# Gate and up projections of a two-block language model: one 512-column matmul in place of two of 256 columns, with the two halves of the bank added by VectorE

## The reference, cut to what matters

```python
def swiglu(h, w_gate_up, w_down):          # h: (1, 256, 1024)
    gu = h @ w_gate_up                     # 1024 x 5632
    gate, up = jnp.split(gu, [D_FF], axis=-1)        # D_FF = 2816
    return (jax.nn.silu(gate) * up) @ w_down         # 2816 x 1024

h = h + hybrid_mixer(rmsnorm(h, norm_mix_w[l]), ...)
h = h + swiglu(rmsnorm(h, norm_ffn_w[l]), w_gate_up[l], w_down[l])     # for l in 0, 1
```

## Time and profile before

| | before |
|---|---|
| median of 3 runs | 2579.13 us (2577.0 to 2579.67) |
| profiled execution, its own time | 2580.57 us |
| span from first to last instruction in it | 2578.8 us |
| PE busy | 2251.0 us (87%) |
| VectorE busy | 1209.9 us (47%) |
| ScalarE busy | 923.3 us (36%) |
| mean granted TensorE clock | 0.947 |

### The profile page before, as it was taken

One profiled execution on the slowest core, in us unless ns is written; L12 is line 12 of the kernel. 1 busy time (PEld: TensorE's weight loads), 2 busy tenths in 40 slices (PEclk: granted clock), 3 DMA queues, 4 the chain that ended last, 5 costly groups with the idle time before them and its releaser, 6 DMA issues.

```text
span 2578.8 us, 37982 instructions
## 1 busy us (share of the span) xinstructions
PE 2251.0 (87%) x16798; PEld 1689.4 (66%) x16798; DVE 1209.9 (47%) x1715; ACT 923.3 (36%) x1315; POOL 1.4 (0%) x6
## 2 busy tenths in 40 slices
PE   8998676667989666676999999999999999999998
PEld 7773122112744221121899999989989999898997
DVE  3543212121873111110565588665456647876554
ACT  4141000001232000000555577554345546865443
POOL 0000000000000000000000000000000000000000
PEclk9999878788999888888999999999999999999999
DMA  7419999999258999999644443445444444344542
GB/s 287 165 58 395 427 428 428 427 428 427 117 249 360 428 428 427 428 427 427 266 164 164 168 159 136 164 179 188 171 180 164 164 150 182 142 154 164 184 176 106
DMA packets 48203, 662.94 MB, mean 257 GB/s; under 512 B 5344, under 2 KB 5600, under 8 KB 7968
## 3 DMA queue, kind: packets, MB, share of 16 engines
q1 hardware_dynamic: 47808, 659.17, 63.6%
q0 software_dynamic: 224, 1.26, 0.1%
HBM read 659.36 MB, written 1.05 MB: 256 GB/s over the span
## 4 chain that ended last, share of the span: by engine, by line
PE 59%; DMA 27%; DVE 6%; ACT 6%; issue 1%; DVEq 0%; SPq 0%; ACTq 0%
DMA ring<-w_dram 27%; PE ps L2476 8%; PE ps L2478 8%; PE ps L2477 8%; PE ps L1932 3%; PE ps L891 3%; PE ps L1355 2%; PE ps L2732 2%; PE ps L2733 2%; PE ps L2734 2%; PE ps L923 2%; PE ps L3340 2%; PE ps L3338 2%; PE ps L3339 2%; ACT r L2453 1%
## 5 line engine op out<-in xcount | busy, mean ns | idle before, releaser
L2464 DVE TENSOR_TENSOR r<-ring,r 128x1024 fp32r<-128x1024 f32 (+2 forms) x376 | 503.9, 1350 | 352.3 <-ACT r L2453 351.7
L2476 PE MATMUL ps<-r 128*128 128x256 f32 x2112 | 607.7, 288 | 5.6 <-DVE r L2536 5.5
L2477 PE MATMUL ps<-r 128*128 128x256 f32 x2112 | 598.6, 283 | 0.0
L2478 PE MATMUL ps<-r 128*128 128x256 f32 x2112 | 598.4, 283 | 0.0
L2453 ACT ACTIVATE r<-ring 128x1024 fp32r<-128x1024 f32 (+2 forms) x376 | 428.5, 1155 | 290.7 <-PE ps L2478 126.9
L891 PE MATMUL ps<-ring 128*32 128x512 f32 x1936 | 298.9, 750 | 180.9 <-DMA ring<-w_dram 180.7
L2476 PEld LDWEIGHTS ps<-r 128*128 128x128 f32 x2112 | 405.2, 192 | 12.3 <-issue 7.3
L2477 PEld LDWEIGHTS ps<-r 128*128 128x128 f32 x2112 | 405.4, 192 | 0.5
L2478 PEld LDWEIGHTS ps<-r 128*128 128x128 f32 x2112 | 405.3, 192 | 0.0
L891 PEld LDWEIGHTS ps<-ring 128*32 128x32 f32 x1936 | 61.4, 124 | 405.1 <-DMA ring<-w_dram 200.9
L1137 DVE TENSOR_TENSOR arena<-ps,arena 128x512 f32<-128x512 f32 x16 | 11.1, 692 | 440.0 <-PE ps L891 440.0
(11 more groups left out here) (446 smaller groups left out, 3067.2 us busy)
## 6 DMA issues: line engine op xcount, KB each, us to landing
ring<-w_dram SPq DMA_DIRECT2D x301, 2048.0 KB, 22.8
arena<-w_dram SPq DMA_DIRECT2D x6, 2048.0 KB, 13.9
ring<-w_dram SPq DMA_DIRECT2D x4, 1024.0 KB, 4.9
arena<-w_dram SPq DMA_DIRECT2D x2, 1536.0 KB, 7.2
x<-x_dram SPq DMA_DIRECT2D x2, 512.0 KB, 3.8
ring<-w_dram SPq DMA_DIRECT2D x2, 512.0 KB, 10.3
out_dram<-x SPq DMA_DIRECT2D x4, 256.0 KB, 2.0
cst<-w_dram SPq DMA_DIRECT2D x1, 973.0 KB, 23.4
```

What stands on the lines that cost most here:

```text
L2464: v.tensor_tensor(lo, w, hi.bitcast(F32), SUB).then_inc(*S.up(f"lo {s}", *(["free " + name] if last else [])))
L2476: pe.matmul(out, hi[:, k, :], K.HH[:, k, :], start=k == 0, stop=False)
L2477: pe.matmul(out, hi[:, k, :], K.HL[:, k, :], start=False, stop=False)
L2478: r = pe.matmul(out, lo[:, k, :], K.HH[:, k, :], start=False, stop=k == 7)
```

## The change

Upper and lower features of a block k become one moving operand of 512 columns (`K.HHL`, a view of the same buffer: two pieces of 256 columns that lie 2048 elements apart). `wide_pe` takes a bank for each tile instead of one for each pair. Its matmul of `hi` by `HHL` writes the whole bank: `hi` by `HH` in the left half, `hi` by `HL` in the right half. `lo` by `HH` is added to the left half by a second matmul of 256 columns. PE doesn't add the two halves; `wide_dve` does, with a copy of the right half to SBUF and an addition of the left half to it, for each tile, with a wait on VectorE's own semaphore between the two. Gate and up thus both pass through VectorE into `FF`, where before ScalarE read the gate and VectorE the up part straight from PSUM. Silu now waits for VectorE's sum of the gate (`g{i} sum`) and reads SBUF, the sums of up wait for Silu, because they overwrite `FF`, and the product is a third pass over `FF` in SBUF, behind one more wait on VectorE's own semaphore. The wait for `f{i-2}` stands now on VectorE as well (its own signal of two chunks ago). ScalarE's wait for `nT6 read` in chunk 0 goes. No transfer is added, taken away or moved in the order.

```diff
--- before.py
+++ after.py
@@ -223,6 +223,7 @@
         self.TMP = sb("tmp", 1536)
         self.CSR = sb("csr", 288, F32R)
         self.HH, self.HL = (R32[:, i * 2048:(i + 1) * 2048].rearrange("p (k t) -> p k t", k=8) for i in range(2))
+        self.HHL = R32[:, 0:4096].rearrange("p (h k t) -> p k h t", h=2, k=8)
         self.WS = [[R32[:, i:i + 2048].rearrange("p (k n) -> p k n", k=8) for i in (j, j + 2048)]
                    for j in (4096, 8192)]
         self.ps = ctx.enter_context(nc.psum_tensor("ps", [128, 8, 512], F32))
@@ -2492,6 +2493,30 @@
             yield
 
 
+def wide_pe(K, pe, S, j, name, first=None):
+
+    for n in range(2):
+        p = bank(K, pe, f"{name}{n}")
+        hi, lo = parts(K, j + n)
+        pe.wait_ge(*K.after(f"lo {j + n}"))
+        for k in range(8):
+            if first and n == 0:
+                wait_features(K, pe, first, k)
+            pe.matmul(half2(p), hi[:, k, :], K.HHL[:, k, :, :], start=k == 0, stop=False)
+            r = pe.matmul(p[:, 0:256], lo[:, k, :], K.HH[:, k, :], start=False, stop=k == 7)
+        r.then_inc(*S.up(f"used {j + n}", f"{name}{n}"))
+
+
+def wide_dve(K, v, S, out, name):
+
+    for n in range(2):
+        p = K.banks[f"{name}{n}"]
+        v.wait_ge(*K.after(f"{name}{n}"))
+        v.tensor_copy(out[:, n, :], p[:, 256:512]).then_inc(*S.up())
+        v.wait_ge(*S.now())
+        v.tensor_tensor(out[:, n, :], p[:, 0:256], out[:, n, :], ADD).then_inc(*S.up(f"{name}{n} read", f"{name} sum"))
+
+
 def proj_beside(K, e, S, j, cut, todo=(), fine=False, last=None):
 
     for n in range(2):
@@ -3320,8 +3345,7 @@
     for i in range(11):
         c = K.first_tile[f"{st}_gu{i}"]
         for j, part in ((0, "g"), (2, "u")):
-            for _ in proj_pe(K, pe, S, c + j, f"{st} {part}{i}", first=None if i or j else st):
-                pass
+            wide_pe(K, pe, S, c + j, f"{st} {part}{i}", first=None if i or j else st)
     acc = {(t, n): bank(K, pe, f"{st} d{t}{n}") for t in range(2) for n in range(2)}
     for i in range(11):
         if i % 2 == 0:
@@ -3350,15 +3374,13 @@
         c = K.first_tile[f"{st}_gu{i}"]
         for _ in proj_beside(K, a, S, c, cut_act):
             pass
-        a.wait_ge(*K.after(f"{st} g{i}"))
+        a.wait_ge(*K.after(f"{st} g{i} sum"))
         if i > 1:
             a.wait_ge(*K.after(f"{st} f{i - 2}"))
-        elif i == 0:
-            a.wait_ge(*K.after(f"{st} nT6 read"))
-        a.activation(b.SG[i % 2], half2(K.banks[f"{st} g{i}"]), ACT.Silu).then_inc(*S.up(f"{st} g{i} read"))
+        a.activation(b.SG[i % 2], b.FF[i % 2], ACT.Silu).then_inc(*S.up(f"{st} silu{i}"))
         for _ in proj_beside(K, a, S, c + 2, cut_act):
             pass
-        a.wait_ge(*K.after(f"{st} u{i} read"))
+        a.wait_ge(*K.after(f"{st} ff{i}"))
         a.activation(b.FH[:, 2 * i:2 * i + 2, :], b.FF[i % 2], ACT.Copy).then_inc(*S.up(f"{st} fh{i}"))
     for i in range(11):
         if i % 2 == 0:
@@ -3372,12 +3394,17 @@
     norm_HL_dve(K, v, st, st + "_gu0")
     for i in range(11):
         c = K.first_tile[f"{st}_gu{i}"]
+        FF = b.FF[i % 2]
         for j in (0, 2):
             for _ in proj_beside(K, v, S, c + j, cut_dve):
                 pass
-        v.wait_ge(*K.after(f"{st} u{i}"))
-        v.wait_ge(*K.after(f"{st} g{i} read"))
-        v.tensor_tensor(b.FF[i % 2], half2(K.banks[f"{st} u{i}"]), b.SG[i % 2], MUL).then_inc(*S.up(f"{st} u{i} read"))
+            if i > 1 and not j:
+                v.wait_ge(*K.after(f"{st} f{i - 2}"))
+            elif j:
+                v.wait_ge(*K.after(f"{st} silu{i}"))
+            wide_dve(K, v, S, FF, f"{st} {'gu'[j // 2]}{i}")
+        v.wait_ge(*S.now())
+        v.tensor_tensor(FF, FF, b.SG[i % 2], MUL).then_inc(*S.up(f"{st} ff{i}"))
         v.wait_ge(*K.after(f"{st} fh{i}"))
         f = slice(2 * i, 2 * i + 2)
         v.tensor_tensor(b.FL[:, f, :], b.FF[i % 2], b.FH[:, f, :].bitcast(F32), SUB).then_inc(*S.up(f"{st} f{i}"))
```

## The result

The changed kernel takes 2585.05 us (median of 20 runs, 2580.31 to 2589.22), the kernel before, run beside it, 2580.82 us (20 runs). The ratio of the two on record is 1.0015, 95% interval 1.0009 to 1.0022: 3.9 us slower, between 2.3 and 5.7 (the plain difference of the medians is 4.2). Slower was forecast, with 7.1 us. The sign and the mechanism hold; the size was 1.8 times what was measured. Twenty runs of each kernel still tell it from nothing.

What follows compares the result with a forecast made beforehand. The VectorE-ScalarE chain, 12.03 us a chunk against PE's 11.31, was to become the bound; with the seam each stage ends 3.56 us late, 2 x 3.56 = 7.1 us, so 2586.2 us, range 2577 to 2593.

Steps and rivals of the forecast that it cites:

- PE's gain: Matmuls of gate and up in ffn0 and ffn1: 0.353 us a block, not 0.360; 2.35 us a stage, 4.7 for both.
- The chain: VectorE and ScalarE taking turns in each gate-and-up chunk: 12.03 us start to start, against PE's 11.31.
- PE's start after a late cut: PE's first matmul behind a wait for VectorE's cut was to start 0.33 us after the cut's end.
- When it bites: Gate-and-up chunks: each eats 0.72 us of PE's slack, which lasts four chunks; from chunk 6 PE waits in each.
- the cushion: PE's slack at tile 7, between the end of VectorE's cut and PE's arrival: 3.2 us.
- Start of the down projection: PE was to start down 0 at 1843.14 us, 1.17 us behind before.
- The seam: Passage to the down projection: chunk 10's evictions delay double-tile cuts; PE 0.83 us later at down 1, 3.56 late at down 2.
- covered turn-taking: Rival: chain under 11.67 us stays hidden, kernel not slower; 2574.4 us, or 2576.4 with a seam cost; chance 0.10.
- free own waits: Rival: VectorE's waits for its own results cost nothing; chain 11.45 us, only the seam remains, 2576.4 us; chance 0.06.
- a slower PE: Rival: the two-piece moving operand slows PE's matmuls; at 0.40 us a block 14 us a stage, 2607 us; chance 0.04.
- The longer chain: Rival: VectorE's small operations take 0.48 us each; chain 12.47 us a chunk, 2595.6 us; chance 0.15.
- the second rival: The rival of free own waits: five times 0.11 us off the chain, said to come to 11.45 us; chance 0.06.

Runs made afterwards that it cites:

- wide_left: Changed kernel's 512-column matmuls, but Silu and product read only the left halves straight from PSUM, right halves left out of the result; ratio 0.9963 to the kernel before.
- all3: Changed kernel with both copies before both additions, ScalarE's cut of tile 4i+5 before Silu, down 1 and 2 cut early; ratio 0.9970 to the kernel before.
- inter: Changed kernel, but for each pair of tiles VectorE does both copies, then both additions; ratio 0.9971 to the kernel before.
- all3b: The kernel all3 run once more, for its interval; ratio 0.9972 to the kernel before.

## Why the prediction was right, and where its size was off

- *PE's gain*: forecast 0.353 us a block, 2.35 us a stage. Measured in the changed kernel 0.347 in ffn0 up to the first hold (5.55 us for the 16 blocks from 1714.30 to 1719.85 is 0.347): a tile takes 2.78 us, a stage would gain 4.6. In ffn1 a tile takes 2.83 us up to the first hold, 0.353 a block, as forecast. The lower figure is also the forecast's own bound, 0.347. Not seen in the time, as forecast, since PE isn't what sets it; wide_left and all3 show it.
  The prediction also gave 0.325 us a block from the page on TensorE of the Trainium skill. That figure takes the page's formula for an isolated matmul, and this is a stream; no block here took less than 0.346.
- *The chain*: forecast 12.03 us a chunk, measured 11.91. Each term is in the rows above: copy to addition 0.44 to 0.45 (0.46, four times), two cuts to the first copy 2.28 and 2.27 (2.30), ScalarE's cut to VectorE's 1.08 and 1.07 (1.09), Silu and FH to ScalarE's cut 0.54 (0.53). No link is off by more than 0.03 us, but together they make 0.12, and nine chunks make 1.1 us a stage. **This is the term that was mis-sized.** A sixth of it was in hand beforehand: the rows give 1.08 for ScalarE's cut to VectorE's (1728.23 to 1729.31), which the sum has twice as 1.09.
- *PE's start after a late cut*: forecast 0.33 us from the one row at hand. Measured: the cut of tile 43 ended at 1834.81 (1833.58 + 1.23) and PE started at 1834.95; down 1, 0.06 us; down 2, 0.05. With a first step 0.08 to 0.11 us longer that is 0.16 to 0.22.
- *When it bites*: forecast from chunk 6 on, at tile 27. In ffn0 the first bracket is at tile 27, 76.1 us into the stage, but tile 23 was held by 0.11 us already. In ffn1 it was 0.17 us at tile 31 and the first bracket at tile 35. That ffn0 fits the forecast nearly to the tile is luck in part: PE ran faster there than forecast (11.10 us a chunk, not 11.31) and the chain was shorter (11.91, not 12.03), so a chunk ate 0.81 us of the cushion in place of 0.72. In ffn1, where PE ran at the forecast's rate, it ate 0.60, and the waits came a chunk or two later.
- *Start of the down projection*: forecast 1.17 us later than before in the stage, measured 0.21 earlier (126.69 against 126.90 us behind the first matmul). Most of the miss is here, 1.38 of 3.56 - 1.99 = 1.57 us a stage; 9 x 0.12 = 1.1 of it are the chain.
- *The seam*: forecast 0.83 and 1.56 us at down 1 and down 2. Measured from down 0 to down 1 6.18 us and on to down 2 7.10, so 0.58 and 1.50 over 5.60. From there on the delay grew by 0.11 once (down 2 took 5.71) and then stayed, nearly as forecast.
- *Rivals*: covered turn-taking, free own waits and a slower PE are each refuted (PE's waits in the trace; inter; wide_left). The longer chain was not there: the small operations took 0.41 to 0.42 us. The sum of the second rival had a slip: five times 0.11 off 12.03 is 11.48, not 11.45; it changes nothing.

VectorE's cuts in chunk 10 and behind it, after the change, for the seam (answers to the earlier trace rows; each double cut ends just before PE's start above):

```profile
1833.58 1.23 DVE L2465 TENSOR_TENSOR r<-ring,r 128x1024 fp32r<-128x1024 f32 x1 [0.26 <-ACT r L2454]
1835.38 2.29 DVE L2465 TENSOR_TENSOR r<-ring,r 128x2048 fp32r<-128x2048 f32 x1 [0.58 <-ACT r L2454]
...
1841.76 2.29 DVE L2465 TENSOR_TENSOR r<-ring,r 128x2048 fp32r<-128x2048 f32 x1 [2.50 <-ACT r L2454]
...
1848.87 2.29 DVE L2465 TENSOR_TENSOR r<-ring,r 128x2048 fp32r<-128x2048 f32 x1 [1.11 <-ACT r L2454]
```

The Trainium skill (page VectorE: DVE Perf Modes, section The DRAIN you can't avoid) says that a semaphore after each operation costs nothing extra. Its figures are for copies that each signal or don't. Here every operation signals, and a copy and the addition that waited for it were 0.45 us apart (1728.70 to 1729.15), an addition and the copy that didn't wait for it 0.35 (1729.15 to 1729.50). So it is the wait for one's own last result that costs 0.1 us, not the signal, and inter shows that it reaches the time. The prediction called its two rows a disagreement with the page; that is too strong, since they differ in the wait and not in the signal.

## What to carry to other kernels

Two engines of which neither is full (here 77% and 43% in the gate-and-up part) can bound a third if they hand work back and forth: lay the relay of one iteration end to end, from start to start, and compare it with the bound engine's iteration, then divide the cushion by the difference to see after how many iterations it bites. Close to balance the answer hangs on hundredths: 0.1 us in a chain of 12 us was worth 1 us a stage here, and 0.5 us turned the sign. The remedy was order, not less work: what an engine can do before a wait belongs before it, and independent work of its own belongs into a wait for its own last result.

## What the runs showed of the hardware that was not expected

The same stream of a 512-column matmul and one of 256 ran at two rates in one trace, without a wait and at the same granted clock of 1.00. In wide_left, ffn0 (from one wide matmul to the ninth behind it):

```profile
1759.76 0.40 PE L2505 MATMUL ps<-r 128*128 128x512 f32 x1
...
1762.94 0.40 PE L2505 MATMUL ps<-r 128*128 128x512 f32 x1
```

and in ffn1 (from one to the eighth behind it):

```profile
2429.88 0.39 PE L2505 MATMUL ps<-r 128*128 128x512 f32 x1
...
2432.65 0.39 PE L2505 MATMUL ps<-r 128*128 128x512 f32 x1
```

3.18 / 9 = 0.353 us a block and 2.77 / 8 = 0.346, which over a stage is 124.62 and 122.32 us to the down projection. all3b had it the other way round (122.31 in ffn0, 124.61 in ffn1). It changes between executions of one kernel and is worth up to 2.3 us a stage.

It can also change within a stage, where PE's stream is held. In the changed kernel's ffn0 a tile took 2.77 to 2.78 us up to the first hold, at tile 23, and tiles 28 and 29, behind a later one, 2.82 to 2.83; in its ffn1 it was 2.82 to 2.83 up to the first hold, at tile 31, and 2.77 at tile 32, right behind it. Gate-and-up parts without a hold kept one rate from tile 1 to their end. Why a stream takes the one or the other was not looked for and stays open.

all3 looks like a third case, with 122.32 us in ffn0 and 123.67 in ffn1, but it is another thing. Tile 0 of its ffn1 took 4.42 us in place of 3.06, all later ones 2.77 to 2.78. The window of its first five blocks, 0.65 us each, shows the granted clock at about half, the lower of its two levels (1.2 GHz):

```profile
2381.86:2385.10 3.24, 3.24 (x11) 2.75 (x11) 3.24 (x7) 3.02 (x6) 0.00 (x0) 0.52 0.00 0
```

In the 1.9 us before (2379.90 to 2381.80) PE was busy for 0.69 us at a clock of 1.00, and from 2385.5 on the clock is 1.00 again. This one stretch cost the 1.35 us; no other stage in these traces has it.
